# Weighted sum of the index heads moved from TensorE to GpSimd, and index pieces placed between the turned groups of a head

## Chip, cores and metric

One Trainium2 chip, one core. The metric is the device time of one execution in microseconds, the median of several runs. The engines: PE (TensorE), ACT (ScalarE), DVE (VectorE), POOL (GpSimd) and SP, which issues the transfers.

## What is computed

One layer for 2048 prompt positions and 64 sample positions: an input projection whose columns feed a pooling mixer, a sparse attention and a cross-attention to 256 memory tokens, then an output projection and a gated feed-forward part with a short convolution. The change lies in the sparse attention. Its index scores decide which keys a query keeps:

```
s = einsum('bthd,bsd->bths', qi, ki)                 # 8 index heads of 32, one shared key
score = einsum('bth,bths->bts', wi, relu(s))         # weighted sum of the heads
score = where(visible, score, -inf)
top_val, top_idx = top_k(score, 256)                 # 144 for the sample
```

The attention of 8 heads then runs over the kept keys.

## The kernel before

The program runs phase after phase: the memory keys and values, the projection, the attention (`phase_attend`), then mixing and feed-forward. In the attention the queries are cut into blocks: blocks 0 to 15 hold 128 prompt queries, block 16 the 64 of the sample. Block n sees S = 128(n+1) keys, block 16 sees 576. Keys are cut into segments of at most 512 columns (`segments`) and into tiles of 128, four tiles to a group (`b.groups`).

A block has nine slots, slots 0 to 7 for the attention heads and slot 8 for the cross-attention. Each engine has its own program, written out in slot order, and semaphores join them. In slot h:

- PE first forms the logits of the next head (`early_logits`, two segments; the others follow inside `head_values`). Then it waits for the exponentials of head h, turns the probabilities group by group (`turn`, line 938) and multiplies the turned tiles with the values (`multiply`, line 970).
- ACT copies each turned group from PSUM (`copy_groups`, line 799), then takes the exponential of the next head (line 1031, for the memory heads line 1035).
- DVE masks the logits of the next head in two parts with their maxima (`mask_logits`, line 1188), and in between does two parts of `pick`: the search for the kept keys of block n+1. `pick` starts with the minimum and maximum of the scores (lines 1075 and 1076), halves the bracket eleven times (a counting pass at line 1084 and two one-column steps), then finds the last places by MAX8 and settles ties. If a row fails, registers are loaded and further passes run.

Index scores of block n+2 are formed during block n, in pieces: a piece is one index head of one segment. `portion` gives each slot a tenth of a block's pieces and slot 8 the rest. For a piece PE forms the raw scores (`raw_index`, line 877) into one of two PSUM halves, ACT applies relu (line 1018) into one of three buffers, and PE multiplies the result by a diagonal matrix of the head's weights and adds it up over the eight heads in PSUM (line 892). After the eighth head ACT copies the sum to `scores` (line 1023). GpSimd only makes the diagonal matrices (line 862), eight per block. On PE the pieces of a slot stand before `head_values`, except the last, which stands after the first two turned groups; on ACT all relus of a slot stand before its copies.

The reading side is strict: `pick(b, 0)` waits for all segments of its block (`seg_kept`) in slot 0 of the block before, after part one of the masking of head 1 and before part two.

## Time and profile before

| what | value |
|---|---|
| median of 3 runs | 3636.48 us (3634.03 to 3639.68) |
| profiled execution | 3637.67 us |
| its span in the trace | 3635.9 us |
| mean granted TensorE clock | 0.956 of full speed |
| PE busy | 3244.8 us, 89% |
| DVE busy | 2270.2 us, 62% |
| ACT busy | 1077.7 us, 30% |
| GpSimd busy | 786.3 us, 22% |

The shares are averages over phases with different limits. Busy time of PE overlaps by the pipelining of its instructions, so intervals between starts tell more than durations. The attention phase runs from about 577 to 1712 us of the span.

### The profile page before, as it was taken

The page shows a single profiled execution, that of the slowest core. Times are in us where ns is not written, and L with a number is a line of the kernel's source. Part 1 is how long each engine was busy: PE and PEld are TensorE (multiplying, and loading weights), DVE is VectorE, ACT ScalarE, POOL GpSimd, SP SyncE. Part 2 cuts the span into 40 slices and gives each one's busy share as a digit, 9 for nine tenths or more (in the row PEclk, how much of TensorE's full clock was granted, in tenths as well). Part 3 has the DMA queues.
Part 4 walks back from the last instruction along what each step waited for, and adds up shares of the span by engine and source line. Part 5 has one row for each costly group of instructions (what it writes and reads, how often), then busy time and mean ns, then how long its engine had stood idle before and what let it go on. Part 6 is the DMA issues. An engine that isn't in the chain of part 4 may idle for free. (4 is left out here: it accounts for less than half of the span.)

```text
span 3635.9 us, 51564 instructions
## 1 busy us (share of the span) xinstructions
PE 3244.8 (89%) x19482; PEld 2928.7 (81%) x19482; DVE 2270.2 (62%) x4788; ACT 1077.7 (30%) x1854; POOL 786.3 (22%) x404
## 2 busy tenths in 40 slices
PE   3899994788899998986989999999888899999997
PEld 2777773567677776775989999999878899999997
DVE  4666762778788777773246666666521666667654
ACT  2222222445455554543222212212121212211211
POOL 0000002110100000000354334334214534334320
PEclk7999996999999999998989999999999999999998
DMA  4222215211111110000312111111122111111101
GB/s 133 70 79 85 93 70 147 69 47 50 34 50 28 29 28 25 23 14 28 118 63 70 35 35 59 45 35 52 53 96 88 41 35 58 46 35 48 56 12 49
DMA packets 164910, 202.68 MB, mean 56 GB/s; under 512 B 27775, under 2 KB 138660, under 8 KB 162596
## 3 DMA queue, kind: packets, MB, share of 16 engines
q1 hardware_dynamic: 164772, 200.90, 17.5%
q8 instruction: 79, 1.29, 0.1%
q14 instruction: 59, 0.48, 0.0%
HBM read 155.61 MB, written 45.25 MB: 55 GB/s over the span
## 5 line engine op out<-in xcount | busy, mean ns | idle before, releaser
L1663 DVE SCALAR_TENSOR_TENSOR ffn_gv<-ffn_up,ffn_taps,ffn_gv 128x1056 f32<-128x1056 f32 (+2 forms) x264 | 418.8, 1600 | 142.0 <-ACT ffn_gv L1616 135.7
L1684 DVE TENSOR_TENSOR feed_hT<-feed_hT,ffn_ps_d 128x352 f32<-128x352 f32 x528 | 275.3, 522 | 329.6 <-PE ffn_ps_d L1569 329.6
L1556 PE MATMUL ffn_ps_u<-feed_nhi,feed_up_hi 128*128 128x352 f32 x2112 | 459.7, 326 | 15.5 <-DVE feed_nlo L1694 11.0
L1556 PE MATMUL ffn_ps_u<-feed_nhi,feed_up_lo 128*128 128x352 f32 x2112 | 456.9, 324 | 0.0
L1556 PE MATMUL ffn_ps_u<-feed_nlo,feed_up_hi 128*128 128x352 f32 x2112 | 456.2, 324 | 0.0
L1556 PEld LDWEIGHTS ffn_ps_u<-feed_nhi,feed_up_hi 128*128 128x128 f32 x2112 | 361.0, 190 | 18.9 <-DVE feed_nlo L1694 12.4
L1569 PE MATMUL ffn_ps_d<-ffn_a_hi,ffn_down_hi 128*128 128x352 f32 x1056 | 344.1, 326 | 29.3 <-DVE ffn_a_lo L1675 23.9
L1556 PEld LDWEIGHTS ffn_ps_u<-feed_nhi,feed_up_lo 128*128 128x128 f32 x2112 | 364.0, 189 | 0.0
L1556 PEld LDWEIGHTS ffn_ps_u<-feed_nlo,feed_up_hi 128*128 128x128 f32 x2112 | 360.2, 188 | 0.0
L862 POOL TENSOR_SCALAR att_diag<-ident,keep_w 128x128 f32<-128x128 f32 (+1 forms) x136 | 80.3, 611 | 1253.7 <-PE att_ps_s L892 740.0
L1569 PE MATMUL ffn_ps_d<-ffn_a_lo,ffn_down_hi 128*128 128x352 f32 x1056 | 343.1, 325 | 0.0
L1569 PE MATMUL ffn_ps_d<-ffn_a_hi,ffn_down_lo 128*128 128x352 f32 x1056 | 342.8, 325 | 0.0
L892 PE MATMUL att_ps_s<-att_relu,att_diag 128*128 128x512 f32 (+12 forms) x672 | 312.2, 549 | 20.3 <-ACT att_relu L1018 19.4
L970 PEld LDWEIGHTS att_ps_o<-att_v,att_pT 128*128 128x128 f32 x2176 | 271.2, 192 | 56.7 <-ACT att_pT L799 43.1
L1188 DVE CUSTOM_DVE_ANT_0 att_probs<-att_ps_l,att_mask 128x512 f32<-128x512 f32 (+10 forms) x336 | 194.3, 602 | 178.6 <-PE att_ps_l L922 171.6
L970 PE MATMUL att_ps_o<-att_v,att_pT 128*128 128x128 f32 x2176 | 286.0, 279 | 18.3 <-ACT att_pT L799 15.2
L1623 ACT ACTIVATE ffn_a_hi<-ffn_gv 128x1056 fp32r<-128x1056 f32 x44 | 47.8, 1087 | 841.6 <-DVE ffn_gv L1673 841.6
L1503 POOL TENSOR_TENSOR feed_up_hi<-feed_raw_up,feed_ones 128x1024 fp32r<-128x1024 f32 x82 | 173.2, 2112 | 460.6 <-PE ffn_ps_u L1556 460.6
L799 ACT ACTIVATE att_pT<-att_ps_p 128x512 f32<-128x512 f32 (+3 forms) x370 | 182.2, 528 | 229.5 <-PE att_ps_p L938 229.3
L1084 DVE TENSOR_SCALAR_CACHE_REDUCE att_work<-att_scores,att_mids 128x384 f32<-128x384 f32 (+14 forms) x165 | 235.7, 1428 | 1.5
L1569 PEld LDWEIGHTS ffn_ps_d<-ffn_a_hi,ffn_down_hi 128*128 128x128 f32 x1056 | 201.1, 190 | 30.2 <-DVE ffn_a_lo L1675 24.5
L1504 POOL TENSOR_TENSOR feed_up_lo<-feed_raw_up,feed_up_hi 128x1024 fp32r<-128x1024 f32 x82 | 217.0, 2646 | 6.4
(258 smaller groups left out, 5932.0 us busy)
## 6 DMA issues: line engine op xcount, KB each, us to landing
feed_raw_up<-in_w_up SPq DMA_DIRECT2D x44, 1024.0 KB, 5.0
scratch_sT<-proj_sT SPq DMA_DIRECT2D x16, 1472.0 KB, 5.2
ffn_raw_down<-in_w_down SPq DMA_DIRECT2D x22, 1024.0 KB, 4.8
feed_nlo<-scratch_mixT SPq DMA_DIRECT2D x16, 528.0 KB, 7.5
proj_x<-in_x_prompt SPq DMA_DIRECT2D x16, 512.0 KB, 4.6
att_qi<-scratch_sT SPq DMA_DIRECT2D x16, 512.0 KB, 3.6
att_qa<-scratch_sT SPq DMA_DIRECT2D x16, 512.0 KB, 5.2
att_qb<-scratch_sT SPq DMA_DIRECT2D x32, 256.0 KB, 5.8
```

The lines of the kernel that those rows point to most:

```text
L799: ins = act.activation(dst, src, ACT.Copy)
L862: ins = pool.tensor_scalar(diag[0:b.T, b.n % 2, h, 0:b.T], ident[0:b.T, 0:b.T], keep["w8"][0:b.T, b.n, h:h + 1], None, ALU.mult)
L892: ins = pe.matmul(ps_s[0:b.T, 0:hi - lo], diag[0:b.T, b.n % 2, h, 0:b.T], relu[0:b.T, count % 3, 0:hi - lo], start=(h == 0), stop=(h == IH ...
L970: ins = pe.matmul(ps_o[0:T, P * slot:P * slot + P], pT[0:hi - lo, seq % 2, k, 0:T], values, start=first, stop=last)
L1084: st.step(dve.tensor_scalar(low_work, row, col(mids, r), None, ALU.is_gt, ALU.add, accum_out=col(counts, r)))
L1188: dve.tensor_tensor_reduce(probs[0:T, seq % 2, lo:hi], ps_l[0:T, (first + s) % 2, 0:hi - lo], mask[0:T, u, lo:hi], 1.0, -3.0e38, ALU.add, ...
L1503: st.step(pool.tensor_tensor(hi, raw, ones[:, 0:1].unsqueeze(1).broadcast_to(list(raw.shape)), ALU.mult))
L1504: pool.tensor_tensor(lo, raw, hi.bitcast(F32), ALU.subtract).then_inc(ready, 1)
L1556: ins = pe.matmul(ps_u[:, half, s, 0:SUB], a[:, q, k, :], b[:, k, SUB * s:SUB * s + SUB], start=(k == 0 and n == 0), stop=(k == KC - 1 and ...
L1569: ins = pe.matmul(ps_d[:, j % 2, 0:SUB], a[:, e, P * c:P * c + P], b[:, e, SUB * s:SUB * s + SUB], start=(e == 0 and n == 0), stop=(e == 1 ...
L1663: ins = dve.scalar_tensor_tensor(gv[:, half, lo:hi], up[:, lo + shift + j - 2:hi + shift + j - 2], taps[:, 2 * j + half, e:e + 1], gv[:, h ...
L1684: dve.tensor_tensor(at, at, ps_d[:, j % 2, 0:SUB], ALU.add).then_inc(partial_read[j % 2], 1)
```

## The change

GpSimd now multiplies four heads at a time by their weights and adds them up in a tree; the diagonal matrices, the weighting matmuls, their PSUM bank and ACT's copy are gone. ACT writes relu into a ring of three buffers of four heads. The pieces of a slot are dealt over its turned groups (`shares`): on PE the share of group g stands after the transposes of group g+1 and before the multiplication of group g, on ACT the relus of the share stand before the copy of group g. On DVE the search gets a different end: the last places are removed by MAX8 and a replacing pass, ties need no table, several one-column steps become scalar instructions, two small tiles lie in PSUM, and the negation of maxima is part of the reduction. More rounds follow for rows more than 8, 16 and 32 places below the bracket. The 1 MB table `falling` is no longer loaded.

```diff
+RING = 3
-        diag = m.sb("diag", [P, 2, IH, P])
-        relu = m.sb("relu", [P, 3, 512])
+        relu = m.sb("relu", [P, RING, 4, 512])
...
+        def shares(b, h):
+
+            other = ahead(b, 2)
+            numbers = portion(other, h) if other else range(0)
+            count = len(b.groups) if h < NH else 2
+            cut = lambda g: -(-len(numbers) * g // count)
+            return [numbers[cut(g):cut(g + 1)] for g in range(count)]
...
-        def copy_groups(act, b, h):
+        def copy_groups(act, b, h, index_relu=None):
 
             count = len(b.groups) if h < NH else 2
             for g in range(count):
+                if index_relu and ahead(b, 2):
+                    index_relu(ahead(b, 2), shares(b, h)[g])
...
-            sp.dma_start(falling[:, :], t["falling"].broadcast_to([P, SEQ])).then_inc(tables_loaded, 16)
...
+            def weigh(b, s, half):
+
+                w = b.segs[s][1] - b.segs[s][0]
+                group = 2 * (segs_before[b.n] + s) + half
+                at = relu[0:b.T, group % RING, :, 0:w]
+                pool.wait_ge(relu_ready, 4 * group + 4)
+                weights = keep["w8"][0:b.T, b.n, 4 * half:4 * half + 4].unsqueeze(2).broadcast_to([b.T, 4, w])
+                st.step(pool.tensor_tensor(at, at, weights, ALU.mult))
+                return at
+
             for b in BLOCKS:
-                if b.n >= 2:
-                    pool.wait_ge(seg_summed, segs_before[b.n - 1])
-                for h in range(IH):
-                    ins = pool.tensor_scalar(diag[0:b.T, b.n % 2, h, 0:b.T], ident[0:b.T, 0:b.T], keep["w8"][0:b.T, b.n, h:h + 1], None, ALU.mult)
-                ins.then_inc(diag_ready, 1)
+                for s, (lo, hi) in enumerate(b.segs):
+                    first_four, last_four = weigh(b, s, 0), weigh(b, s, 1)
+                    pool.tensor_tensor(last_four, first_four, last_four, ALU.add).then_inc(paired, 1)
+                    pool.wait_ge(paired, segs_before[b.n] + s + 1)
+                    st.step(pool.tensor_tensor(last_four[:, 0:2], last_four[:, 0:2], last_four[:, 2:4], ALU.add))
+                    if s == 0 and b.n >= 2:
+                        pool.wait_ge(scores_taken, b.n - 1)
+                    pool.tensor_tensor(scores[0:b.T, b.n % 2, lo:hi], last_four[:, 0], last_four[:, 1], ALU.add).then_inc(seg_kept, 1)
...
                 for g in range(len(groups)):
                     if g + 1 < len(groups):
                         turn(g + 1)
-                    if g == 0:
-                        index_pieces(other, numbers)
+                    index_pieces(ahead(b, 2), shares(b, h)[g])
                     if rest:
                         segment_logits(*rest.pop(0))
                     ins = multiply(g)
...
-                    act.activation(relu[0:T, i % 3, 0:hi - lo], ps_i[0:T, i % 2, 0:hi - lo], ACT.Relu).then_inc(relu_ready, 1)
+                    if i % 4 == 0 and group >= RING:
+                        before = group - RING
+                        act.wait_ge((paired, seg_kept)[before % 2], before // 2 + 1)
+                    act.activation(relu[0:T, group % RING, i % 4, 0:hi - lo], ps_i[0:T, i % 2, 0:hi - lo], ACT.Relu).then_inc(relu_ready, 1)
...
-                        st.step(dve.scalar_tensor_tensor(col(mids, r + 1), col(back), col(steps, r), col(mids, r), ALU.subtract, ALU.add))
+                        st.step(dve.tensor_scalar(col(mids, r + 1), col(back), col(steps, r), col(mids, r), ALU.subtract, ALU.add))
...
-                    st.step(dve.tensor_scalar(low_work, row, col(bound), -FAR, ALU.is_gt, ALU.mult))
+                    st.step(dve.tensor_scalar(low_work, row, col(bound), None, ALU.is_gt, ALU.add, accum_out=col(above)))
                 elif part == HALVINGS + 2:
 
-                    st.step(dve.tensor_tensor(low_work, low_work, row, ALU.add))
-                    st.step(dve.max(top[0:T, :], low_work))
+                    st.step(dve.scalar_tensor_tensor(low_work, low_work, -FAR, row, ALU.mult, ALU.add))
                     st.step(dve.tensor_scalar(col(place), col(above), -1.0, b.keep - 1.0, ALU.mult, ALU.add))
+                    take_next(b, st, 0)
                 elif part == HALVINGS + 3:
-                    st.step(dve.scalar_tensor_tensor(low_work, row, col(kth), falling[0:T, 0:S], ALU.is_equal, ALU.mult))
-                    st.step(dve.max(lowest[0:T, 0:8], low_work))
+                    leave_out_rest(b, st)
+                    st.step(dve.tensor_scalar(col(failed), col(place), 7.5, None, ALU.is_gt))
                 else:
-                    keep_to_tie(b, st, 8)
                     with dve.If(failed_rows(st) > 0):
-                        more_ties(b)
+                        more_places(b)
...
+            def take_next(b, own, start):
+
+                T, left = b.T, work[0:b.T, 0:b.S]
+                own.step(dve.max(top[0:T, :], left))
+                own.step(dve.tensor_scalar(beyond[0:T, :], places[0:T, start:start + 8], place[0:T, 0:1], NEVER, ALU.is_gt, ALU.mult))
+                own.step(dve.tensor_tensor(wanted[0:T, :], top[0:T, :], beyond[0:T, :], ALU.subtract))
+                own.step(dve.match_replace(left, wanted[0:T, :], left, -FAR))
+
+            def leave_out_rest(b, own):
 
                 T, S = b.T, b.S
+                own.step(dve.tensor_scalar(mask[0:T, b.n % 2, 0:S], work[0:T, 0:S], -0.5 * FAR, MASKED, ALU.is_gt, ALU.mult))
+                if not b.sample:
+                    own.step(dve.memset(mask[0:CHUNK, b.n % 2, S - CHUNK:S], MASKED))
...
+            def more_places(b, starts=(8,), more=(16, 24)):
+
                 own = Steps(dve, tie_steps)
+                for start in starts:
+                    take_next(b, own, start)
+                leave_out_rest(b, own)
...
-                st.step(dve.tensor_reduce(neg[0:T, u, h:h + 1], peaks[0:T, seq % 2, 0:len(b.segs)], AX.X, ALU.max))
-                dve.tensor_scalar(neg[0:T, u, h:h + 1], neg[0:T, u, h:h + 1], -1.0, None, ALU.mult).then_inc(neg_ready, 1)
+                dve.tensor_reduce(neg[0:T, u, h:h + 1], peaks[0:T, seq % 2, 0:len(b.segs)], AX.X, ALU.max, negate=True).then_inc(neg_ready, 1)
```

The order on PE in slot 1 of block 12 (S = 1664, so four groups of 4, 4, 4 and 1 tiles; `att_ps_i` raw index scores of block 14, `att_ps_s` their weighted sum, `att_ps_p` turned probabilities, `att_ps_o` values, `att_ps_l` logits of the next head). Before:

```order
L877 MATMUL att_ps_i<-att_kiT,att_qi 128x480
L892 MATMUL att_ps_s<-att_relu,att_diag 128x480
L877 MATMUL att_ps_i<-att_kiT,att_qi 128x480
L892 MATMUL att_ps_s<-att_relu,att_diag 128x480
L938 MATMUL att_ps_p<-ident,att_probs 128x128 x8
L877 MATMUL att_ps_i<-att_kiT,att_qi 128x480
L892 MATMUL att_ps_s<-att_relu,att_diag 128x480
L921 MATMUL att_ps_l<-att_kT,att_qa 128x416
L922 MATMUL att_ps_l<-att_kT,att_qb 128x416
L970 MATMUL att_ps_o<-att_v,att_pT 128x128 x4
L938 MATMUL att_ps_p<-ident,att_probs 128x128 x4
```

With the change, the same stretch and on to the end of the slot:

```order
L946 MATMUL att_ps_p<-ident,att_probs 128x128 x8
L902 MATMUL att_ps_i<-att_kiT,att_qi 128x480
L929 MATMUL att_ps_l<-att_kT,att_qa 128x416
L930 MATMUL att_ps_l<-att_kT,att_qb 128x416
L978 MATMUL att_ps_o<-att_v,att_pT 128x128 x4
L946 MATMUL att_ps_p<-ident,att_probs 128x128 x4
L902 MATMUL att_ps_i<-att_kiT,att_qi 128x480
L929 MATMUL att_ps_l<-att_kT,att_qa 128x416
L930 MATMUL att_ps_l<-att_kT,att_qb 128x416
L978 MATMUL att_ps_o<-att_v,att_pT 128x128 x4
L946 MATMUL att_ps_p<-ident,att_probs 128x128
L902 MATMUL att_ps_i<-att_kiT,att_qi 128x480
```

The weighting matmuls are gone, and the pieces that stood before the transposes now stand one to a group, behind the transposes of the next group.

The order on ACT in the same slot (`att_pT` is the copy of a turned group). Before:

```order
L1018 ACTIVATE att_relu<-att_ps_i 128x480 x3
L799 ACTIVATE att_pT<-att_ps_p 128x512 x3
L799 ACTIVATE att_pT<-att_ps_p 128x128
L1031 ACTIVATE att_probs,att_sums<-att_probs,att_neg 128x1664
```

With the change:

```order
L1024 ACTIVATE att_relu<-att_ps_i 128x480
L809 ACTIVATE att_pT<-att_ps_p 128x512
L1024 ACTIVATE att_relu<-att_ps_i 128x480
L809 ACTIVATE att_pT<-att_ps_p 128x512
L1024 ACTIVATE att_relu<-att_ps_i 128x480
L809 ACTIVATE att_pT<-att_ps_p 128x512
L809 ACTIVATE att_pT<-att_ps_p 128x128
L1032 ACTIVATE att_probs,att_sums<-att_probs,att_neg 128x1664
```

Each relu now stands directly before the copy of a group.

## Rows read from the trace of the kernel before

**Rows 1.** Busy time by stage, block 10.
```profile
core 0: us, PE busy (x) PEld busy (x) DVE busy (x) ACT busy (x) POOL busy (x), PEclk, DMA share, GB/s
1142.00:1221.00 79.00, 75.23 (x449) 59.03 (x447) 61.91 (x154) 45.23 (x88) 4.66 (x8) 1.00 0.12 33
```
**Rows 2.** Groups of instructions, 560 to 1712 us: busy us, mean ns, then idle before.
```profile
L892 PE MATMUL att_ps_s<-att_relu,att_diag 128*128 128x512 f32 (+12 forms) x672 | 312.2, 549 | 20.3 <-ACT att_relu L1018 19.4
```
**Rows 3.** Timeline (start, duration), block 12, head 5: first piece, first transpose.
```profile
1355.55 0.19 PEld L877 LDWEIGHTS att_ps_i<-att_kiT,att_qi 128*128 128x128 f32 x1
...
1358.10 0.14 PEld L938 LDWEIGHTS att_ps_p<-ident,att_probs 128*128 128x128 f32 x1 [0.21 <-issue]
```
**Rows 4.** Timelines of PE and ACT, 1291 to 1329 us: the handoffs.
```profile
1291.14 0.37 PE L877 MATMUL att_ps_i<-att_kiT,att_qi 128*128 128x448 f32 x1
...
1291.54 0.54 ACT L1018 ACTIVATE att_relu<-att_ps_i 128x448 f32<-128x448 f32 x1 [0.94 <-PE att_ps_i L877]
...
1327.99 0.57 ACT L1018 ACTIVATE att_relu<-att_ps_i 128x480 f32<-128x480 f32 x1
1328.44 1.09 ACT L799 ACTIVATE att_pT<-att_ps_p 128x512 f32<-128x512 f32 x2
...
1309.71 1.08 ACT L799 ACTIVATE att_pT<-att_ps_p 128x512 f32<-128x512 f32 x2 [0.53 <-PE att_ps_p L938]
...
1310.36 1.16 PE L970 MATMUL att_ps_o<-att_v,att_pT 128*128 128x128 f32 x8
1311.36 0.60 PE L938 MATMUL att_ps_p<-ident,att_probs 128*128 128x128 f32 x4
1311.71 0.44 PE L921 MATMUL att_ps_l<-att_kT,att_qa 128*128 128x416 f32 x1
```
**Rows 5.** Timeline of ACT: exponentials of blocks 7, 10, 11 and 13.
```profile
944.32 1.15 ACT L1031 ACTIVATE att_probs<-att_probs,att_neg 128x1024 f32<-128x1024 f32 x1
...
986.17 0.48 ACT L1035 ACTIVATE att_probs<-att_ps_l,att_neg 128x256 f32<-128x256 f32 x1
...
1148.87 1.46 ACT L1031 ACTIVATE att_probs<-att_probs,att_neg 128x1408 f32<-128x1408 f32 x1
...
1204.73 0.47 ACT L1035 ACTIVATE att_probs<-att_ps_l,att_neg 128x256 f32<-128x256 f32 x1
...
1217.46 1.58 ACT L1031 ACTIVATE att_probs<-att_probs,att_neg 128x1536 f32<-128x1536 f32 x1 [1.07 <-DVE att_neg L1196]
...
1228.02 1.57 ACT L1031 ACTIVATE att_probs<-att_probs,att_neg 128x1536 f32<-128x1536 f32 x1
...
1421.68 1.78 ACT L1031 ACTIVATE att_probs<-att_probs,att_neg 128x1792 f32<-128x1792 f32 x1
...
1494.93 0.47 ACT L1035 ACTIVATE att_probs<-att_ps_l,att_neg 128x256 f32<-128x256 f32 x1
```
**Rows 6.** Timeline of POOL in the feed-forward phase.
```profile
2242.85 3.60 POOL L1503 TENSOR_TENSOR ffn_down_hi<-ffn_raw_down,feed_ones 128x2048 fp32r<-128x2048 f32 x1 [18.66 <-PE ffn_ps_d L1569]
2246.53 4.61 POOL L1504 TENSOR_TENSOR ffn_down_lo<-ffn_raw_down,ffn_down_hi 128x2048 fp32r<-128x2048 f32 x1
```
**Rows 7.** Timelines of DVE and POOL where both work.
```profile
2208.17 1.89 POOL L1503 TENSOR_TENSOR feed_up_hi<-feed_raw_up,feed_ones 128x1024 fp32r<-128x1024 f32 x1 [7.22 <-PE ffn_ps_u L1556]
...
2208.20 1.89 DVE L1658 COPY ffn_up<-feed_hist 128x2 f32 x1 [0.22 <-DVE ffn_taps L1648]
...
1393.62 4.27 POOL L862 TENSOR_SCALAR att_diag<-ident,keep_w 64x64 f32<-64x64 f32 x8 [90.20 <-PE att_ps_s L892]
...
1394.05 2.03 DVE L1145 MAX8 att_lowest<-att_mask 128x8 f32<-128x1792 f32 x1
```
**Rows 8.** Timeline of DVE: the first reduction of a pick.
```profile
1304.56 2.02 DVE L1075 TENSOR_REDUCE att_low<-att_scores 128x1 f32<-128x1792 f32 x1
```
**Rows 9.** Busy time by stage, columns as in rows 1: PE after its stop.
```profile
1400.00:1404.00 4.00, 0.00 (x0) 0.00 (x0) 0.52 (x3) 0.00 (x0) 0.00 (x0) 0.50 0.00 0
1404.00:1408.00 4.00, 3.04 (x11) 2.46 (x12) 2.38 (x9) 0.00 (x0) 0.00 (x0) 0.50 0.00 0
```
**Rows 10.** Timeline of DVE: its first mask of the attention.
```profile
607.30 0.17 DVE L1067 MEMSET att_mask<- 128x128 f32 x1 [36.03 <-DMA att_falling<-in_falling]
```

More of the change, by code:

```diff
@@ L939, in turn_group, with head_values @@
                 ins.then_inc(turned, 1)
-            def head_values(b, h, other, numbers, after):
+            def head_values(b, h, after):
                 u, T = b.n % 2, b.T
@@ L997, in _ @@
             for b, h, after in slots():
-                other = ahead(b, 2)
-                numbers = portion(other, h) if other else range(0)
-                late = numbers[-1:] if h else range(0)
                 if after:
                     early_logits(*after)
-                index_pieces(other, numbers[:len(numbers) - len(late)])
                 if h == 0 and b.n:
                     rows_turned(BLOCKS[b.n - 1])
-                head_values(b, h, other, late, after)
+                head_values(b, h, after)
             rows_turned(BLOCKS[NB])
@@ L1039, in _ @@
             for b in BLOCKS[0:2]:
-                for part in range(NHEADS):
-                    index_relu(b, part)
+                index_relu(b, range(IH * len(b.segs)))
             exponentials(BLOCKS[0], 0)
             for b, h, after in slots():
-                if ahead(b, 2):
-                    index_relu(ahead(b, 2), h)
                 if h == 0 and b.n:
                     copy_groups(act, BLOCKS[b.n - 1], 9)
-                copy_groups(act, b, h)
+                copy_groups(act, b, h, index_relu)
                 if after:
@@ L1112, in pick @@
-                    st.step(dve.max(lowest[0:T, 0:8], low_work))
+                    leave_out_rest(b, st)
+                    st.step(dve.tensor_scalar(col(failed), col(place), 7.5, None, ALU.is_gt))
                 else:
-                    keep_to_tie(b, st, 8)
                     with dve.If(failed_rows(st) > 0):
-                        more_ties(b)
+                        more_places(b)
                     dve.memset(idle[:, :], 0.0).then_inc(scores_taken, 1)
                     dve.wait_ge(scores_taken, b.n + 1)
-            def keep_to_tie(b, own, found):
-                T, S = b.T, b.S
-                row, at, order = scores[0:T, b.n % 2, 0:S], mask[0:T, b.n % 2, 0:S], work[0:T, 0:S]
-                own.step(dve.scalar_tensor_tensor(chosen[0:T, 0:found], places[0:T, 0:found], missing[0:T, 0:1], lowest[0:T, 0:found], ALU.is_equal, ALU.mult))
-                own.step(dve.tensor_reduce(last_tie[0:T, 0:1], chosen[0:T, 0:found], AX.X, ALU.add))
-                own.step(dve.tensor_scalar(at, order, last_tie[0:T, 0:1], MASKED, ALU.is_lt, ALU.mult))
-                own.step(dve.scalar_tensor_tensor(at, row, kth[0:T, 0:1], at, ALU.is_le, ALU.mult))
-                own.step(dve.tensor_scalar(failed[0:T, 0:1], last_tie[0:T, 0:1], 0.5, None, ALU.is_lt))
@@ L1137, in failed_rows @@
                 return dve.snap(parts[0] + parts[1] + parts[2] + parts[3])
-            def more_ties(b):
-                T, S = b.T, b.S
-                at, order = mask[0:T, b.n % 2, 0:S], work[0:T, 0:S]
+            def more_places(b, starts=(8,), more=(16, 24)):
                 own = Steps(dve, tie_steps)
-                own.step(dve.match_replace(at, lowest[0:T, 0:8], order, 0.0))
-                own.step(dve.max(lowest[0:T, 8:16], at))
-                keep_to_tie(b, own, 16)
+                for start in starts:
+                    take_next(b, own, start)
+                leave_out_rest(b, own)
+                own.step(dve.tensor_scalar(failed[0:b.T, 0:1], place[0:b.T, 0:1], starts[-1] + 7.5, None, ALU.is_gt))
                 total = failed_rows(own)
```

91 lines of the change are left out of this document (35 added, 56 removed).

## The prediction

> **What bounds the kernel now.** I read the span in 40 slices first, because the edit lies in the attention phase alone (about 577 to 1712 us), and the later phases keep their code. Then busy time by stage: in block 10 PE is busy 75.2 of 79 us at full clock, the vector engine 61.9, ACT 45.2 and GpSimd 4.7 [rows 1]. So PE sets the pace, and the vector engine is the next limit. Third, the groups of instructions: 672 weighting matmuls keep PE 312 us (0.55 each) [rows 2]. Fourth, the order in time: in head 5 of block 12 PE spends 1355.55 to 1358.10, 2.55 us, on two index pieces before its first transpose [rows 3]. Last, the handoffs between PE and ACT, because the edit puts the pieces between them.
>
> **PE and ACT inside a head (slots 1 to 7 of a block).** Removed: the weighting matmuls and the stretch in front. Added: raw piece, relu, and only then the copy of the turned group. In the order above the copy of group g follows relu of its share, whose raw matmul follows the transposes of group g+1. Before, copy and transposes overlapped. The chain from rows [rows 4]: raw to relu 0.40 (1291.14 to 1291.54), relu to the next copy 0.45 (1327.99 to 1328.44), copy to multiply 0.65 (1309.71 to 1310.36): 1.5 us, in which PE has at most one segment of logits (0.4). A multiply of four tiles takes 1.0 (1310.36 to 1311.36), four transposes 0.35.
>
> Block 10 (three groups, of 4, 4 and 3 tiles, three pieces a slot): two groups turned 0.7 plus 0.1 to start, 1.5, multiply 1.0, turn three 0.25, 1.5, 1.0, 1.5, multiply three 0.75, logits of the next head 0.8: 9.1 us. The slot with four pieces takes 0.45 more. Seven slots: 64.2. Before they took 1204.73 - 1148.87 = 55.9 [rows 5]: **+8.3**. Block 7 (two groups, two or three pieces): 0.8 + 1.5 + 1.0 + 1.5 + 1.0 + 0.8 = 6.6, or 7.05; seven slots 47.6 against 986.17 - 944.32 = 41.9: **+6**. Block 13 (three full groups and a pair, 512 wide): 10.2, and 12.0 with the fourth piece, whose relu stands before the last copy: 73.2 against 73.3: **0**, since the removed work pays for the waits. By the same walk: blocks 4 and 5 (16 pieces instead of 24) +5 together, 6 and 7 +12, 8 and 9 (24 pieces in three groups) +6, 10 and 11 (32 pieces) +15, 12 and 13 +1. Block 14 (16 small pieces) is bound by the vector engine and stays; blocks 0 to 3 and 15, with one group or no pieces, gain 1 to 2 each, 8. Sum **+31**.
>
> **The new chain on GpSimd (slot 0).** GpSimd ran no such sum before; the nearest rows are its multiply by a broadcast operand, 3.60 us for 2048 a partition, and its subtract of two full ones, 4.61 [rows 6]. From zero to these would be 0 to 17 us for the last half segment; the shapes are nearly the same, so I take them. A 448-wide segment: after its last relu one multiply of 4x448 (3.2), an add of 4x448 (4.1), of 2x448 (2.1) and of 448 (1.1), with gaps 10.8 us; 512 wide 12.2, 416 wide 10.1. Where the last slot holds seven of 32 pieces (blocks 10 to 13), GpSimd still sums the segment before when they come: 2.5 more in the next block. Before, one matmul and one copy followed that relu.
>
> The vector engine asks for these scores in slot 0 of the next block, between its two parts of masking head 1. With three or four segments, head 1's exponential waits for part two. So from exp of head 0 to exp of head 1, in block 11: 12.0 (scores) + two reductions like that of 2.02 [rows 8] and the small steps 4.5 + masking 0.85 = 17.3, against 1228.02 - 1217.46 = 10.6 [rows 5]: +6.7. Blocks 8 to 14 so: 5.4, 6.0, 6.4, 6.7, 7.7, 8.4, 10, in sum 50. Up to two segments mask head 1 before asking, and a slot or more covers the wait: 12 over blocks 1 to 7. I take **+60**, a little under the 62, as part lies under PE's own slot. Queued behind the wait are the search passes and the mask of every later head; behind them ACT's exponentials and PE.
>
> The Trainium skill ("GPSIMD Engine Reference", section on elementwise performance) speaks against the move: 4.5 us for a 2048-element two-input add, about half the vector engine's rate, hence elementwise work belongs there. The trace agrees (4.61); by the page's rate for the multiplies too, slot 0 would cost some 7 us more over all blocks.
>
> **The last slot.** It had seven pieces ahead of its transposes, each at 0.96 us, and a long tail of the pick. From the memory exp to the next block's exp was 1217.46 - 1204.73 = 12.7 in block 10 [rows 5]. Now: exps 1.9, transposes 0.8, first relu after 0.5, four relus at 0.5, copy to multiply 0.65, multiply 1.0, three more pieces 1.9, last copy 0.5: 9.3. Sum over the blocks, without 12: **-42**. The shorter pick (two full passes, a masking pass and some ten small steps of 0.15 to 0.25 fewer, against one pass counted at single instead of double rate) is what lets it fall; in slots 1 to 7 it is hidden under PE. In block 12 the search for block 13 fails: from the reference's inputs I work out one row 16 places below its bracket, so the new code makes three more rounds of pass and replace (2 x 2.03 each [rows 7]) and two more register checks where the old made one: **+8**. Block 7's search has a row at place 10 and stays at one extra round.
>
> **The start.** The first mask waited for the table that is gone [rows 10]; its 1 MB also stood before the next index queries: **-3.5**. The first GpSimd sums lie under the loads of the queries.
>
> **Clock.** When PE stood still from 1392 to 1404 us its granted clock was 0.50, the 1.2 GHz level, and stayed there after it restarted [rows 9]. Seven blocks now leave PE idle for 5 to 8 us in slot 0: between nothing and 4 us each; I take +1 each, **+8**.
>
> The sum: 31 + 60 - 42 + 8 - 3.5 + 8 = **+61.5**. The profiled execution took 3637.7 us (span 3635.9), 1.2 above the median shown. So 3637.7 + 61.5 = 3699; taken as **3695**, 1.6% slower. A measurement of this kernel tells 0.2% (7 us) from no change.
>
> **The rivals.**
> *The removed work wins.* If relu and copy keep out of each other's way, slots fall to the vector engine's pace: for block 10 two search passes (2.35 each: [rows 8] scaled to 1536 columns, and 0.6 of small steps) and 2.0 of masking, 6.7 instead of 8.0. Seven such slots in the five blocks 9 to 13 give back 45 instead of costing 31; the late scores cost the same: 3637.7 - 45 + 60 - 42 + 8 - 3.5 = **3615**. For it: 312 us of matmuls really go. Against it: the order on ACT. It decides at about 0.5 us per piece of waiting instead of 1.1. Chance 0.18.
> *The port.* A copy of 128x2 took 1.89 us while a GpSimd multiply that began 0.03 us before took 1.89 [rows 7]: a two-column copy sat out the whole instruction. If the search passes suffer likewise, 165 passes wait on average 1 us: **3860**. Against it: the MAX8 over 1792 columns, with one input, took 2.03 while GpSimd worked [rows 7], as long as it takes alone. It decides if a pass with its count, or a step on one column, is held. The Trainium skill ("SBUF — State Buffer", section on who interferes with whom) says the same: an exclusive lock against two-input instructions and the two-port modes, not against a scalar pass that writes its count; by it each block has only the masking pass and one two-input pass exposed, 2 x 1.5 us, mostly under PE's time. Chance 0.06.
> *Nothing moves.* Waits and savings cancel, within 7 us of 3637. For it: costs of 107 and savings of 45 (the terms above by sign), each uncertain by a third. Chance 0.06.
> The forecast, 3645 to 3755, has 0.70.
>
> **How the numbers follow.** Slower 0.70 + 0.06 = 0.76, same 0.06, faster 0.18. The unknown costs spread the forecast: waits inside a head 0.4 to 1.9 us a piece instead of 1.5 (-60 to +25), the GpSimd chain at 0.7 to 1.3 of its size (-25 to +25), the clock 0 to 28. The range 3600 to 3755 leaves out the port (0.06), a third of the first rival (0.06) and the ends of the forecast (0.06).
>
> **What would show it.** In the new trace: slots 1 to 7 of block 10 at about 9.1 us, copies that start 0.45 us after a relu, PE idle on ACT before each first multiply; GpSimd busy 500 to 600 us in the phase, 3.4 us for 4x480 multiplied; the reduction at the head of each pick waiting 6 to 10 us for a GpSimd sum; the last slot at 9 to 10 us. Wrong, if slots are at 7 us with ACT free, if the reduction doesn't wait, or if the counting passes are longer than 2.1 us at 1792 columns.

## The result, and the profile after

The changed kernel takes **3758.97 us** (median of 4 runs, 3752.3 to 3767.2), the kernel before, run beside it, 3637.73 (4 runs, 3634.0 to 3639.7). The ratio is 1.0336, with a 95% interval of 1.0319 to 1.0352: 121 us, or 3.4%, slower. The prediction had the direction and half the size, and its range ended 4 us below. The profiled execution took 3752.3 us (span 3750.4), 114.6 more than that of before. It was the fastest of the four, which span 15 us, so differences of a few us between this profile and another can be ordinary spread.

Block 10, the stage of [rows 1], by the same view of busy time:
```profile
core 0: us, PE busy (x) PEld busy (x) DVE busy (x) ACT busy (x) POOL busy (x), PEclk, DMA share, GB/s
1211.00:1308.00 97.00, 66.19 (x383) 53.52 (x383) 58.05 (x136) 42.82 (x86) 52.76 (x21) 0.91 0.10 27
```
PE has 9 us less to do than in [rows 1] and takes 18 us longer, so something else than PE's work sets its pace. GpSimd is busy for 53 of 97 us, and PE's granted clock is down to 0.91. The groups of GpSimd's instructions (busy us, mean ns; then idle time before them) sum to 551 us:
```profile
L876 POOL TENSOR_TENSOR att_relu<-att_relu,keep_w 128x2048 f32<-128x2048 f32 (+12 forms) x84 | 256.9, 3058 | 1107.7 <-ACT att_relu L1024 1107.4
L882 POOL TENSOR_TENSOR att_relu<-att_relu 128x2048 f32<-128x2048 f32 (+12 forms) x42 | 160.8, 3828 | 3.3
L884 POOL TENSOR_TENSOR att_relu<-att_relu 128x1024 f32<-128x1024 f32 (+12 forms) x42 | 86.4, 2058 | 3.3
L887 POOL TENSOR_TENSOR att_scores<-att_relu 128x512 f32<-128x512 f32 (+12 forms) x42 | 47.3, 1125 | 3.3
```
The view of waits over the attention phase (us in total, times, longest) names two that matter:
```profile
PE att_ps_o L978 <- ACT att_pT L809: 250.6, 267, 1.4
...
DVE att_failed L1071 <- POOL att_scores L887: 90.3, 15, 9.8
```
The first is PE's multiply waiting for a copy of turned tiles. The same row of the kernel before:
```profile
PE att_ps_o L970 <- ACT att_pT L799: 23.2, 37, 1.2
```
The second is new: the vector engine waits for GpSimd's scores once in each of 15 blocks.

One head of block 10 in order of time (PE and ACT; start, duration), to be read against the handoffs of [rows 4]:
```profile
1239.88 1.04 PE L946 MATMUL att_ps_p<-ident,att_probs 128*128 128x128 f32 x8
...
1240.67 0.43 PE L902 MATMUL att_ps_i<-att_kiT,att_qi 128*128 128x416 f32 x1
...
1241.14 0.52 ACT L1024 ACTIVATE att_relu<-att_ps_i 128x416 f32<-128x416 f32 x1 [1.49 <-PE att_ps_i L902]
...
1241.55 0.59 ACT L809 ACTIVATE att_pT<-att_ps_p 128x512 f32<-128x512 f32 x1
1242.20 1.16 PE L978 MATMUL att_ps_o<-att_v,att_pT 128*128 128x128 f32 x8 [0.67 <-ACT att_pT L809]
...
1243.19 0.49 PE L946 MATMUL att_ps_p<-ident,att_probs 128*128 128x128 f32 x3
...
1243.44 0.43 PE L902 MATMUL att_ps_i<-att_kiT,att_qi 128*128 128x416 f32 x1
1243.91 0.52 ACT L1024 ACTIVATE att_relu<-att_ps_i 128x416 f32<-128x416 f32 x1 [1.76 <-PE att_ps_i L902]
...
1244.32 0.59 ACT L809 ACTIVATE att_pT<-att_ps_p 128x512 f32<-128x512 f32 x1
1244.97 1.16 PE L978 MATMUL att_ps_o<-att_v,att_pT 128*128 128x128 f32 x8 [1.10 <-ACT att_pT L809]
```
From raw score to multiply it is 1240.67 to 1242.20 and 1243.44 to 1244.97: 1.53 us, twice. The copy's input has been there since the transposes ended, but its relu stands ahead of it on ACT.

Slot 0 of the same block (ACT, GpSimd and the vector engine):
```profile
1209.74 1.08 ACT L1024 ACTIVATE att_relu<-att_ps_i 128x512 f32<-128x512 f32 x2 [1.48 <-PE att_ps_i L902]
1210.97 3.60 POOL L876 TENSOR_TENSOR att_relu<-att_relu,keep_w 128x2048 f32<-128x2048 f32 x1 [0.71 <-ACT att_relu L1024]
...
1214.65 4.52 POOL L882 TENSOR_TENSOR att_relu<-att_relu 128x2048 f32<-128x2048 f32 x1
...
1219.25 2.36 POOL L884 TENSOR_TENSOR att_relu<-att_relu 128x1024 f32<-128x1024 f32 x1
...
1221.69 1.26 POOL L887 TENSOR_TENSOR att_scores<-att_relu 128x512 f32<-128x512 f32 x1
1223.02 0.09 DVE L1071 MEMSET att_failed<- 128x32 f32 x1 [7.95 <-POOL att_scores L887]
```
The last relu ended at 1210.82, the sum at 1222.95: 12.1 us for 512 columns, the 12.2 of the forecast. The vector engine stood for 7.95 of them.

The exponentials on ACT, which mark the slots as in [rows 5]:
```profile
1211.19 1.48 ACT L1032 ACTIVATE att_probs<-att_probs,att_neg 128x1408 f32<-128x1408 f32 x1
...
1228.12 1.47 ACT L1032 ACTIVATE att_probs<-att_probs,att_neg 128x1408 f32<-128x1408 f32 x1 [3.13 <-DVE att_neg L1189]
...
1238.09 1.47 ACT L1032 ACTIVATE att_probs<-att_probs,att_neg 128x1408 f32<-128x1408 f32 x1
...
1247.14 1.47 ACT L1032 ACTIVATE att_probs<-att_probs,att_neg 128x1408 f32<-128x1408 f32 x1
...
1257.68 1.47 ACT L1032 ACTIVATE att_probs<-att_probs,att_neg 128x1408 f32<-128x1408 f32 x1
...
1297.52 0.48 ACT L1036 ACTIVATE att_probs<-att_ps_l,att_neg 128x256 f32<-128x256 f32 x1
...
1307.74 1.58 ACT L1032 ACTIVATE att_probs<-att_probs,att_neg 128x1536 f32<-128x1536 f32 x1
```
Slot 0 took 16.9 us (1211.19 to 1228.12), slots 1 to 7 took 69.4, the last slot 10.2. The same reading of every block gives the balance below (us, one profiled execution each, blocks 0 to 15):

| part | before | after | change | forecast |
|---|---|---|---|---|
| slot 0 | 143.8 | 193.9 | +50 | +60 |
| slots 1 to 7 | 710.9 | 801.1 | +90 | +31 |
| last slot | 204.9 | 192.7 | -12 | -34 |
| first exponential | 608.4 | 604.3 | -4 | -3.5 |
| last block and later phases | | | -9.5 | 0 |
| clock, as a term of its own | | | not separate | +8 |
| sum | | | +114.6 | +61.5 |

### The profile page after: what moved, and what is told of

Its sections match the earlier page's. It is cut to its first block and busy times, and to the rows that moved or that the text cites. A ratio compares the mean times of both kernels' runs of the same rounds, so it can differ in the third digit from the quotient of the medians.

```text
span 3750.4 us, 50121 instructions
## 1 busy us (share of the span) xinstructions
PE 3109.9 (83%) x18810; PEld 2857.9 (76%) x18810; DVE 2215.1 (59%) x4561; ACT 1048.8 (28%) x1812; POOL 1257.2 (34%) x478
## 5 line engine op out<-in xcount | busy, mean ns | idle before, releaser
L876 POOL TENSOR_TENSOR att_relu<-att_relu,keep_w 128x2048 f32<-128x2048 f32 (+12 forms) x84 | 256.9, 3058 | 1107.7 <-ACT att_relu L1024 1107.4
L978 PE MATMUL att_ps_o<-att_v,att_pT 128*128 128x128 f32 x2176 | 334.6, 300 | 226.9 <-ACT att_pT L809 221.9
L978 PEld LDWEIGHTS att_ps_o<-att_v,att_pT 128*128 128x128 f32 x2176 | 283.8, 202 | 308.1 <-ACT att_pT L809 307.1
L1024 ACT ACTIVATE att_relu<-att_ps_i 128x512 f32<-128x512 f32 (+12 forms) x336 | 171.5, 527 | 550.8 <-PE att_ps_i L902 549.6
L1082 DVE TENSOR_SCALAR_CACHE_REDUCE att_work<-att_scores,att_mids 128x384 f32<-128x384 f32 (+14 forms) x165 | 235.7, 1428 | 1.5
L1496 POOL TENSOR_TENSOR ffn_down_hi<-ffn_raw_down,feed_ones 128x2048 fp32r<-128x2048 f32 x22 | 81.2, 3689 | 425.8 <-PE ffn_ps_d L1562 425.8
L946 PE MATMUL att_ps_p<-ident,att_probs 128*128 128x128 f32 (+2 forms) x1264 | 202.0, 296 | 22.4 <-ACT att_probs L1032 12.9
```

The source lines that it names most:

```text
L876: st.step(pool.tensor_tensor(at, at, weights, ALU.mult))
L946: ins = pe.transpose(ps_p[0:width, e, P * i:P * i + T], src, ident[0:T, 0:T])
L978: ins = pe.matmul(ps_o[0:T, P * slot:P * slot + P], pT[0:hi - lo, seq % 2, k, 0:T], values, start=first, stop=last)
L1024: act.activation(relu[0:T, group % RING, i % 4, 0:hi - lo], ps_i[0:T, i % 2, 0:hi - lo], ACT.Relu).then_inc(relu_ready, 1)
L1082: st.step(dve.tensor_scalar(low_work, row, col(mids, r), None, ALU.is_gt, ALU.add, accum_out=col(counts, r)))
L1496: st.step(pool.tensor_tensor(hi, raw, ones[:, 0:1].unsqueeze(1).broadcast_to(list(raw.shape)), ALU.mult))
```

## The experiments

Medians of at least 4 runs; the kernel before took 3637 to 3641 us beside them. "Slots 1 to 7" are sums over blocks 0 to 15.

| run | what it is | us | ratio to before, 95% | slot 0 | slots 1 to 7 | last slot |
|---|---|---|---|---|---|---|
| | before | 3638 | | 144 | 711 | 205 |
| | changed | 3759 | 1.032 to 1.035 | 194 | 801 | 193 |
| 1 | sharing-out undone | 3597 | 0.987 to 0.990 | 167 | 676 | 181 |
| 2 | copy ahead of relus | 3658 | 1.003 to 1.006 | 181 | 699 | 203 |
| 3 | changed, scores early | 3735 | 1.025 to 1.029 | 186 | 838 | 137 |
| 4 | before + vector edits | 3623 | 0.994 to 0.997 | 140 | 712 | 191 |
| 5 | changed, masking first | 3766 | 1.033 to 1.037 | 170 | 832 | 191 |
| 6 | changed, waits filled | 3758 | 1.032 to 1.035 | 191 | 812 | 185 |
| 7 | 1 + scores early | 3581 | 0.982 to 0.985 | 152 | 673 | 178 |
| 8 | 7 + last relu behind copy | 3546 | 0.973 to 0.976 | 156 | 646 | 173 |
| 9 | changed, slot 0 filled | 3782 | 1.037 to 1.041 | 198 | 820 | 196 |
| 10 | 8, masking first | 3585 | 0.984 to 0.987 | 151 | 685 | 173 |
| 11 | 8 with a ninth a slot | 3581 | 0.982 to 0.986 | 170 | 685 | 158 |
| 12 | 2 + scores early | 3546 | 0.973 to 0.976 | 176 | 643 | 168 |

**Run 1: the sharing-out undone.**
```diff
 # PE
-index_pieces(ahead(b, 2), shares(b, h)[g])          # ahead of multiply(g)
+index_pieces(other, numbers[:len(numbers) - len(late)])   # ahead of head_values; the last piece behind turn(1)
 # ACT
-copy_groups(act, b, h, index_relu)
+index_relu(ahead(b, 2), portion(ahead(b, 2), h))
+copy_groups(act, b, h)
```


> The changed kernel with one part undone: the raw index scores of a slot stand again in front of the head's transposes on PE (the last one behind them), and all their relus in front of the copies on ACT. GpSimd still sums the heads. Theory (the chain raw score, relu, copy, multiply, passed once for each group, is what lengthened slots 1 to 7): slots of block 10 fall from 10.2 us to about 7.3, since PE then has 6.2 us of work and the vector engine 6.7; slots 1 to 7 of all blocks lose most of their 87 us, the last slot gets some 10 us back; time about 3670. Rival (slots are long because PE runs at its lower clock, or because GpSimd's traffic disturbs the others): slots of block 10 stay above 9 us, time above 3730.

3596.6 us: 162 less than the changed kernel, 43 less than before and 73 less than the theory expected. Slots 1 to 7 lost 125 us, slot 0 lost 27, and the last slot fell by 12 where 10 more were expected. The exponentials of block 10:
```profile
1156.27 1.46 ACT L1037 ACTIVATE att_probs<-att_probs,att_neg 128x1408 f32<-128x1408 f32 x1
...
1162.71 1.46 ACT L1037 ACTIVATE att_probs<-att_probs,att_neg 128x1408 f32<-128x1408 f32 x1
...
1169.17 1.47 ACT L1037 ACTIVATE att_probs<-att_probs,att_neg 128x1408 f32<-128x1408 f32 x1
...
1176.48 1.46 ACT L1037 ACTIVATE att_probs<-att_probs,att_neg 128x1408 f32<-128x1408 f32 x1
```
6.4, 6.5, 7.3 us: the pace of two search passes and three maskings that the first rival was priced at (6.7). GpSimd's work is the same here (544 us in these blocks), so neither it nor its traffic was what made the slots 9 to 10 us long. The wait of PE's multiplies falls from 250.6 to 98.3 us.

**Run 2: the copy ahead of the relus of its share, on ACT alone.**
```diff
 for g in range(count):
-    if index_relu and ahead(b, 2):
-        index_relu(ahead(b, 2), shares(b, h)[g])
     ...
     ins.then_inc(copied[e], 1)
+    if index_relu and ahead(b, 2):
+        index_relu(ahead(b, 2), shares(b, h)[g])
```


> The changed kernel with the order on ACT turned round inside each share: copy of the turned group first, then the relus of the group's share. PE's order is as changed. Theory (the copy waiting for relu of its share is the cost): each first multiply starts about 0.8 us after its transposes instead of 2, slots of block 10 at 6.8 to 7.5 us, time about 3655. Rival (PE is held by the relus through the two score buffers, whatever the order): a share's second and third raw scores wait for the relu behind the copy, slots stay above 8.5 us, time above 3715.

3657.9 us, as the theory had it. With two lines moved on one engine, slots 1 to 7 lose 102 us, and the wait of PE's multiplies for a copy all but goes:
```profile
PE att_ps_o L978 <- ACT att_pT L807: 14.2, 43, 0.5
```
The profile is still 58 us longer than that of run 1. Of these, 22 lie in the last slot, 14 in slot 0 and 13 in slot 1 of blocks 1 to 7 (59.5 us in sum; 46.8 in run 1, 51.6 changed, 28.1 before). The scores are a part of it: each share's relus now end later, and the vector engine waits 113.9 us for them, against 90.3 in the changed kernel and 59.6 in run 1.

**Run 3: the scores early.**
```diff
-        SHARE = 10
+        SHARE = 8
```


> The changed kernel with the index pieces dealt over slots 0 to 7 alone (an eighth each, none in the memory slot). Theory (slot 0 is long because the vector engine waits for GpSimd's sum of the last segment): that wait, 90 us in all, falls below 15, slot 0 of blocks 8 to 14 falls by 5 to 8 us each; the last slot loses its pieces too (-10); slots 1 to 7 get a quarter more pieces (+15); time about 3715. Rival (slot 0 is long for the pieces and the low clock, and the wait is hidden behind PE): slot 0 of block 10 stays above 14 us, time above 3745.

3735.3 us, between the two expectations. The wait for scores in block 10 falls from 7.95 us to this:
```profile
1191.38 0.09 DVE L1071 MEMSET att_failed<- 128x32 f32 x1 [1.63 <-POOL att_scores L887]
```
In all it falls from 90.3 to 5.6 us. Slot 0 of blocks 8 to 14 falls by 23 us in sum (to 93), not by 5 to 8 each; the last slot loses 56, and slots 1 to 7 gain 37, more than twice what was expected. That fits a chain of 1.5 us for each added piece; no run isolates it.

**Run 4: the vector engine's edits alone,** on the kernel before; its `pick`, `take_next`, `leave_out_rest`, `more_places` and `mask_logits` are those of the change, the weighting stays on PE.


> The kernel before with only the vector engine's edits: the shorter end of the search, negated maxima, the table that is gone; weighting stays on PE and the order is the one before. The two small results of the search's end that the change keeps in PSUM are in SBUF here. Theory (the last slot is set by the search's tail on the vector engine): -3.5 at the start, the last slot 3 us shorter in nine blocks, +8 for the extra rounds of the search for block 13: about 3620. Rival (the last slot is set by PE's seven pieces, so that the shorter tail buys nothing by itself): 3636 to 3644.

3623.4 us, 17 less than before. The time is the theory's, but the place is not. The last slot loses 14 us in sum: 16 in blocks 6, 14 and 15, 2 in blocks 8 to 11 and 13 together and 2 in the other small ones, and it gets 6.5 more in block 12. In blocks 8 to 11 and 13 the shorter search bought next to nothing by itself, as the rival had it. Taken in this order, the parts of the change come to -17 (vector edits), -27 (GpSimd in place of PE, run 1 against run 4) and +162 (sharing-out).

**Run 5: head 1's second masking ahead of the wait for scores.**
```diff
-if h < 8 and not b.sample:
+if h and h < 8 and not b.sample:
     pick(ahead(b, 1), 2 * h)
 if after:
     mask_logits(*after, 1)
+if h == 0 and not b.sample:
+    pick(ahead(b, 1), 0)
```


> The changed kernel with one pair exchanged on the vector engine, in slot 0 alone: the second part of masking head 1 goes ahead of the first step of the search (which waits for GpSimd's scores). Theory (head 1's exponential is late because its masking is queued behind that wait): slot 0 of blocks 8 to 14 falls by 5 to 7 us each; a part comes back in slot 1, where the search is late; time 3759 - 25 to 40, so 3720 to 3734. Rival (the whole row of work behind the wait is what counts, and the vector engine only waits in another place): slot 0 and slot 1 together stay within 2 us, time above 3750.

3765.9 us: the rival. The runs of the two kernels overlap (3762 to 3768 and 3752 to 3767), so no difference is shown. In blocks 8 to 14 slot 0 falls from 116 to 87 us and slot 1 rises from 67 to 89, 1 us less for a pair; the wait was moved, not hidden. So "head 1 is queued behind the wait" told where the time showed, not what it cost.

**Run 6: PE's waits filled.**
```diff
-far, beyond = ps_far[:, 0:HALVINGS + 1], ps_far[:, 32:40]
+far, beyond = m.sb("far", [P, HALVINGS + 1]), m.sb("beyond", [P, 8])
...
+pe.matmul(ps_far[0:T, 0:448], qa[:, u, 0, 0:T], kT[:, 0, 0:448], start=True, stop=True)
 ins = multiply(g)
```


> The changed kernel with one more matmul of 448 columns ahead of each group's multiply, at the place where PE waits for the copy; its result goes nowhere (and two small results of the search's end lie in SBUF instead of PSUM). About 370 matmuls of 0.4 us, 150 us of PE work. Theory (a good part of the slots' excess over 9.1 us is the lower granted clock that follows PE's gaps): granted clock of blocks 8 to 12 rises from 0.89 to 0.96 up to 0.97 or more, slots of block 10 fall from 10.2 to 9.3, time 3735 or less in spite of the work. Rival (the clock costs little; the slots are long by their waits alone): the added work is hidden or not, slots of block 10 stay at 10 us or more, time 3755 to 3850.

3758.1 us. The 369 added matmuls took 404 ns each, as expected, but overlapped with their neighbours: PE's busy time over blocks 0 to 15 rose from 805 to 852 us only. The granted clock of blocks 9 to 11 rose from 0.94, 0.91 and 0.93 to 0.98, 0.96 and 0.98, and slots 2 to 7 of block 10 fell from 59.4 to 56.5 us, near the walk's 9.1 each. But over blocks 8 to 13 these slots fell by 4 us only, and blocks 12 to 15 took 15 us longer. Neither theory is right as written: a higher clock came with slots 4 us shorter in sum over blocks 8 to 13, and the added work cost as much again elsewhere.

**Run 9: only slot 0 filled** (the small results in SBUF, as in run 6).
```diff
 seq = NHEADS * b.n + h
+if h == 1 and 8 <= b.n <= 13:
+    for i in range(18):
+        pe.matmul(ps_far[0:T, 0:448], qa[:, u, 0, 0:T], kT[:, 0, 0:448], start=True, stop=True)
 pe.wait_ge(exp_done, seq + 1)
```


> The changed kernel with 18 matmuls of 448 columns (3.6 to 4 us) in slot 0 of blocks 8 to 13, where PE stands idle until head 1's exponential; their result goes nowhere (and two small results of the search's end lie in SBUF). Theory (the gap in slot 0 is what takes the clock down, and the slots of blocks 10 to 12 that are over the walk's 9.1, 9.7 and 10 are the price): slots 1 to 7 of blocks 8 to 13 lose 8 to 14 us of their 404, slot 0 stays, time 3745 to 3751. Rival (the short waits inside each slot take it down, or the price is nothing): the sum of these slots stays within 4 us, time 3755 to 3765.

3781.5 us, outside both. Slots 2 to 7 of blocks 8 to 13 fell by 3.5 us again, and slot 1 rose by 13: the added matmuls stood in front of work that had come. Another 16 us lie in blocks 2 to 6, where no matmul was added: 309 us at a mean granted clock of 0.75, against 294 at 0.82 in the changed kernel's profile. The code there is not the same, though. Runs 6 and 9 keep two small results of the search in SBUF, the changed kernel has them in PSUM, and in SBUF their instructions can stand while GpSimd works (block 4, GpSimd and the vector engine):
```profile
769.13 2.75 POOL L876 TENSOR_TENSOR att_relu<-att_relu,keep_w 128x1536 f32<-128x1536 f32 x1 [1.61 <-ACT att_relu L1027]
...
769.71 2.19 DVE L1114 TENSOR_SCALAR att_beyond<-att_places,att_place 128x8 f32<-128x8 f32 x1
```
The step over 8 columns ended when the multiply did (771.90 and 771.88). In the changed kernel the longest of these 19 steps took 0.23 us. The vector engine is busy 6 us longer in blocks 2 to 6 of run 9 than in the changed kernel. How the other 10 us divide between what follows from these stops, the clock and ordinary spread isn't settled.

**Run 7: run 1 with the scores early** (`SHARE = 8`).


> The kernel of the first run of this study (sharing-out undone, 3597 us) with the index pieces dealt over slots 0 to 7 alone. Theory (what is left of GpSimd's cost is the wait for its last segment in slot 0 and, in blocks 2 to 7, in slot 1): slot 0 of block 10 falls from 16.1 to 12, slot 1 of blocks 2 to 6 from 7 to 9 us down to 4 to 5; time about 3565. Rival (GpSimd, which needs 3.3 us a half segment and so 6.6 of each slot of 6.5 with four pieces, is now the bound and stays late): time above 3590.

3581.3 us, between the two expectations. Slot 0 of block 10 fell to 10.9 and slot 1 of blocks 1 to 7 from 46.8 to 30.1 us in sum, as expected. But slots 2 to 7 of blocks 8 to 13 rose from 256 to 277: with four pieces in each slot, four relus stood ahead of the first copy. (GpSimd needs 551 / 84 = 6.6 us for a half segment of four pieces, not the 3.3 of the expectation; its 6.6 us a slot are right.)

**Run 8: run 7 with the last relu behind the first copy.**
```diff
-index_relu(ahead(b, 2), portion(ahead(b, 2), h))
-copy_groups(act, b, h)
+index_relu(ahead(b, 2), numbers[:len(numbers) - len(late)])
+copy_groups(act, b, h, index_relu, late)     # relu of late, after the copy of group 0
```


> The kernel of the run before (sharing-out undone, pieces over slots 0 to 7) with one order changed on ACT: the relu of a slot's last piece, whose raw score follows the transposes on PE, goes behind the copy of the first group instead of ahead of it. Theory (PE still waits 98 us for copies, mostly for the first): those waits fall by half, but slots of blocks 9 to 13 are at the vector engine's pace and stay; blocks 3 to 8 gain 0.3 us a slot: 10 to 15 us less than the run before. Rival (PE's waits lie beside the vector engine's time everywhere): within 5 us of it.

**3546.3 us**, 35 less than run 7 and 2.5% faster than the kernel before; more than twice the gain expected, and 21 us of it in slots 2 to 7 of blocks 9 to 13, which were expected to stay. The slots came back to 256 us, and their exponentials now wait for the vector engine, which is the bound in these slots:
```profile
1129.82 1.47 ACT L1039 ACTIVATE att_probs<-att_probs,att_neg 128x1408 f32<-128x1408 f32 x1 [0.58 <-DVE att_neg L1199]
...
1136.54 1.48 ACT L1039 ACTIVATE att_probs<-att_probs,att_neg 128x1408 f32<-128x1408 f32 x1 [0.93 <-DVE att_neg L1199]
...
1143.25 1.48 ACT L1039 ACTIVATE att_probs<-att_probs,att_neg 128x1408 f32<-128x1408 f32 x1 [1.01 <-DVE att_neg L1199]
```
**Run 10: run 8 with the exchange of run 5.**


> The kernel of the last run before this (sharing-out undone, pieces over slots 0 to 7, last relu behind the first copy; 3546 us) with head 1's second masking ahead of the search's first step, as in the exchange tried on the changed kernel. Theory (with the scores there in time, the two reductions alone, 4 us, stand ahead of head 1's exponential, and PE idles for them in slot 0): slot 0 of blocks 8 to 13 falls from 10 to 11 us to 7, slot 1 gives back 2: time 3530. Rival (the vector engine is the bound in these blocks, so that its order doesn't matter): within 6 us of 3546.

3585.4 us, 39 more: neither. The vector engine's rows in slot 0 of block 10 show why:
```profile
1132.58 0.65 DVE L1192 CUSTOM_DVE_ANT_0 att_probs<-att_ps_l,att_mask 128x468 f32<-128x468 f32 x1 [3.02 <-PE att_ps_l L930]
...
1133.41 1.75 DVE L1083 TENSOR_REDUCE att_low<-att_scores 128x1 f32<-128x1536 f32 x1
```
The third segment's logits come late from PE; in run 8 the two reductions filled that wait of 3 us, here they start behind it. Slots 0 and 1 of block 10 are together 3.3 us longer. Over the phase the vector engine's wait for logits grew from 125 to 154 us, which is most of the 39. On the engine that bounds, the order decided.

**Run 11: run 8 with `SHARE = 9`.**


> The 3546 us kernel with a ninth of the pieces in each of slots 0 to 7 and the rest, four of 32, in the last slot. Theory (GpSimd, at 3.3 us a half segment, needs the time of the last slot to be in time): the wait for scores comes back by 2 to 4 us in each of blocks 2 to 14, time 3560 to 3580. Rival (GpSimd is in time with room to spare, and fewer pieces in slots 1 to 7 help): 3535 to 3545.

3580.9 us, 1 above the theory's span: the wait for scores is back with 66 us (13 times, 5 us each where 2 to 4 were expected), slot 0 is 14 us longer in sum, and slot 1 of blocks 1 to 7 16 us longer. GpSimd needs the last slot's time for its sum.

**Run 12: run 2 with the scores early.**


> The changed kernel, its pieces still shared out over the groups, with the copy of each group ahead of the relus of its share on ACT and the pieces dealt over slots 0 to 7. Theory (it was the order on ACT and the late scores that cost, and not where on PE the raw scores stand): within 12 us of the 3546 us kernel. Rival (spreading the raw scores over the groups costs by itself, since the last share's relus end a slot later than the next exponential could start): time above 3570.

3546.3 us, the same as run 8. The pieces are still shared out over the groups on PE, and that costs nothing once each copy goes ahead of its share's relus, the scores are in time and no piece stands in the last slot. PE's wait for copies is 12 us:
```profile
PE att_ps_o L978 <- ACT att_pT L807: 12.1, 38, 0.5
```
## Why the direction was right and the size wrong

**Held.** The chain raw score, relu, copy, multiply was forecast at 1.5 us and measured at 1.53; an undisturbed slot of block 10 at 9.1 and measured at 9.05 (1238.09 to 1247.14); GpSimd's chain at 12.2 for 512 columns and measured at 12.1; its total at 500 to 600 us and measured at 551; slot 0 of blocks 8 to 14 at +50 and measured at +43; the start at -3.5 and measured at -4.

**The port rival fell,** in its large form: the 165 counting passes took 235.7 us, mean 1428 ns, in both kernels. A small form of it is there, though: two passes a block at the end of the search are longer beside GpSimd. The masking passes at the end of the search, in run 4, where GpSimd only makes the diagonal matrices, and in the changed kernel:
```profile
L1118 DVE TENSOR_SCALAR att_mask<-att_work 128x1792 f32<-128x1792 f32 (+14 forms) x18 | 14.4, 799 | 0.7
...
L1118 DVE TENSOR_SCALAR att_mask<-att_work 128x1792 f32<-128x1792 f32 (+14 forms) x18 | 26.2, 1458 | 0.7
```
That is 12 us more of the vector engine's time, and 2 more in the two-input passes (20.6 and 22.7 us). What it costs in device time no run shows. Run 1 has 34 us in the masking passes and is 162 us faster than the changed kernel, so it was not what made the change slow.

**The step that failed is the sum for slots 1 to 7,** +31 forecast and +90 measured. Its walk was laid over blocks 7, 10 and 13 and carried to the others by groups and pieces. Its terms of +5, +12, +6, +15, +1 and 0 (blocks 4 and 5, 6 and 7, and so on to 12 and 13, then 14) measured +14.5, +19, +12, +25, +7.5 and +2. What stood in place of its figures:

- Blocks 0 to 3 and 15, "with one group or no pieces", were to gain 8 us and lost 10. Slot 1 of block 2 went from 2.9 to 7.7 us: the first search pass stands ahead of head 2's masking on the vector engine, and began only when the scores came, as these rows of the changed kernel show.
```profile
690.96 0.09 DVE L1071 MEMSET att_failed<- 128x32 f32 x1 [7.29 <-POOL att_scores L887]
690.97 0.68 DVE L1073 TENSOR_REDUCE att_low<-att_scores 128x1 f32<-128x512 f32 x1
...
693.05 0.75 DVE L1082 TENSOR_SCALAR_CACHE_REDUCE att_work<-att_scores,att_mids 128x512 f32<-128x512 f32 x1
...
694.39 0.56 DVE L1182 CUSTOM_DVE_ANT_0 att_probs<-att_ps_l,att_mask 128x384 f32<-128x384 f32 x1
...
695.18 0.62 ACT L1032 ACTIVATE att_probs<-att_probs,att_neg 128x384 f32<-128x384 f32 x1 [3.14 <-DVE att_neg L1189]
```
- The same holds for blocks 1 to 7 together: "a slot or more covers the wait" priced it at 12 us. Slot 1 rose by 23.5 and slot 0 by 7.4, 31 in all. Slot 1 there falls from 46.8 us in run 1 to 30.1 in run 7, and from 59.5 in run 2 to 27.0 in run 12, when the scores come in time (28.1 before). In the changed kernel itself they took it from 51.6 to 39.5 only (run 3), with more pieces in the slot. So the late scores were the main cause. The cover that was named is one slot of 3 to 5 us, against a wait of 7.29 in the rows above.
- In blocks 8 to 13 slots 2 to 7 rose by 37 us. The walk gives about 19 of them (six sevenths of 6 + 15 + 1). Runs 6 and 9 took 4 us back with a fuller PE, the lower clock's part as far as they show it. The remaining 14 are not explained one by one. In block 10 three slots took 10.5 to 10.7 beside those at 9.1; run 6 left one of the three. Turning the order on ACT alone took slots 2 to 7 of these blocks from 348 to 258 us, below the 310 of before (run 2), so whatever the 14 are, they go with that order.

**The clock** was given 8 us from GpSimd's gap in slot 0. The granted clock fell more widely than that: from 1.00 to 0.91 in block 10 [rows 1], and from 0.96 to 0.71 in block 2. But the lower clock did not make the slots long: run 2 has the same 0.91 in block 10, with slots 2 to 7 at 6.2 to 7.7 us (9.0 to 10.7 changed), its mean over blocks 8 to 13 is 0.88 against 0.93, and run 8, the fastest, has 0.93. Its price in the changed kernel stays open: 4 us in blocks 8 to 13 by runs 6 and 9, unknown in the small blocks. The prediction also read its rows too widely: of PE's stop from 1393.5 to 1404.9 us only the end is at 0.50, the stretch from 1396 to 1400 has a mean of 0.83.

**The last slot** was forecast at -42 + 8 and gave -12. Blocks 8 to 11, 13 and 14 fell by 16 us in sum, block 10 to 10.2 where 9.3 was forecast. Blocks 0 to 7 rose by 2, to 90, in place of falling. Run 2, with the order on ACT turned, has them at 92, and run 1, with the pieces again ahead of the transposes on PE, at 69, though its scores are late too. So in that slot it was the place of the pieces on PE that cost, as far as these two show. The extra rounds in block 12 cost 4 here, 6.5 in run 4 and 12 in runs 1 and 2.

**Luck in the sum.** The slots were 59 us too low and the last slot 22, slot 0 was 10 too high and the clock's term, which lies in the slots, 8. The block of the sample took 6 us less and the later phases 4 less, which the prediction had at nothing; without that the result would have been further off.

**The rivals.** "The removed work wins" had its mechanism right: with the relus kept out of the copies' way, slots of block 10 fell to 6.2 to 7.4 us (run 1), by the vector engine's pace at which it was priced. It was given 0.18 because of the order on ACT, and that order is just what decided: run 2 turns it round with two lines. "Nothing moves" was off by 121 us.

The Trainium skill ("GPSIMD Engine Reference", section on elementwise performance) holds elementwise work to be the vector engine's. Its rate agrees with this trace: 4.52 us for the add of 2048 elements. No run here gives the sum to the vector engine, so its comparison of the two engines is not tested. Taken as advice against GpSimd it would have misled: moving the sum from PE to GpSimd gained 27 us (run 1 against run 4), and 77 with the pieces and the last relu set right (run 8 against run 4), where GpSimd was idle and PE was the bound.

## What to carry to other kernels

An idle engine may take work from the bounding one at a higher price (here 551 us of GpSimd for 312 of PE), if its result is in time. Find out first when the result is wanted and end its inputs early enough (`SHARE = 8`), then look at who waits. When a new producer and consumer pair is dealt into an existing handoff between two engines that work in program order, put the old pair's step first on the engine that both share: two lines on ACT were worth 101 us, and 189 where the scores were early (run 12 against run 3). A wait covered "by a slot" must be compared with the shortest such slot, block by block, and not with the one that was walked through.

## What the runs showed that was not expected

The 369 matmuls of run 6, 149 us by their own rows, added 47 us to PE's busy time: a matmul's row overlaps with the next one's, so the cost of added work is to be read from start to start. The granted clock rose with the filled waits, and nothing was gained in all (run 6). A step of the vector engine over 8 columns took 0.23 us with its result in PSUM and up to 2.19 in SBUF beside a GpSimd multiply (run 9), so an experiment that moves a small tile to make room changes more than it seems to. And one exchange of two steps made no difference clear of noise on the changed kernel (run 5) but cost 39 us on the fastest one (run 10), where the vector engine had become the bound.
